# Reordering a down projection's operand splits around the next projection's block splits, on one Trainium2 core

## The reference

```python
def swiglu(h, w_gate_up, w_down):
    gu = h @ w_gate_up
    g, u = gu[..., :D_FF], gu[..., D_FF:]
    return (jax.nn.silu(g) * u) @ w_down

def shared_kv(x, kv_norm_g, w_kv_s):
    kv = rms_norm(x, kv_norm_g) @ w_kv_s
    k = kv[..., :H_B * DH_B] ...   # and v from the other half

for i in range(DEPTH):             # DEPTH = 2
    h = rms_norm(x, norm_mix_g[i])
    if i < N_A_LAYERS:  mix = diff_attn_layer(h, ...)
    else:               k_s, v_s = shared_kv(x, ...); mix = stick_breaking_layer(h, k_s, v_s, ...)
    x = x + mix
    x = x + swiglu(rms_norm(x, norm_ffn_g[i]), w_gate_up[i], w_down[i])
```

## Time and profile before

| | |
|---|---|
| time, median of 3 runs (lowest, highest) | 1648.55 us (1645.99, 1650.98) |
| the profiled execution's own time | 1650.5 us |
| its span | 1648.6 us |
| mean granted clock of TensorE | 0.995 |
| PE busy | 1618.5 us (98%) |
| PEld busy | 1486.4 us (90%) |
| DVE busy | 1162.8 us (71%) |
| ACT busy | 753.4 us (46%) |
| POOL busy | 216.5 us (13%) |

### The profile page before, as it was taken

How to read it: one execution, slowest core, us unless ns; L and a number is a source line. 1 busy time by engine, 2 the same in 40 slices (tenths; PEclk the granted TensorE clock), 3 DMA queues, 4 the chain that set the end, 5 groups by cost and what they waited for, 6 DMA issues and landing times.

```text
span 1648.6 us, 31629 instructions
## 1 busy us (share of the span) xinstructions
PE 1618.5 (98%) x13132; PEld 1486.4 (90%) x13132; DVE 1162.8 (71%) x1605; ACT 753.4 (46%) x1264; POOL 216.5 (13%) x191
## 2 busy tenths in 40 slices
PE   9999999999999999999899999999999999999999
PEld 8888766699999999999899897667999999999999
DVE  5765477667984797488786337778679848974874
ACT  6444476765541354144555214657555413531441
POOL 0000000023220011012344100000231200110110
PEclk9999999999999999999999999999999999999999
DMA  7133899931222122222234458997412221221222
GB/s 286 67 118 138 349 419 419 419 132 52 103 77 103 52 82 99 76 78 90 90 115 169 165 212 349 419 418 314 167 59 95 90 90 52 103 102 53 78 103 90
DMA packets 40252, 267.54 MB, mean 162 GB/s; under 512 B 4400, under 2 KB 4784, under 8 KB 10928
## 3 DMA queue, kind: packets, MB, share of 16 engines
q1 hardware_dynamic: 36720, 252.95, 39.8%
q0 software_dynamic: 3392, 12.58, 2.1%
HBM read 249.79 MB, written 15.73 MB: 161 GB/s over the span
## 4 chain that ended last, share of the span: by engine, by line
PE 84%; DVE 8%; DMA 3%; ACT 3%; issue 3%; SPq 0%; DVEq 0%; ACTq 0%
PE ps L812 29%; PE ps L608 25%; PE ps L278 4%; PE ps L279 4%; PE ps L280 4%; PE ps L1285 3%; PE ps L1344 2%; PE ps L1226 2%; DVE s_lo L761 2%; PE ps L1263 2%; PE ps L635 2%; PE ps L1248 2%; DMA kv<-in_v_a 1%; DMA xT<-in_v_a 1%; DVE t L775 1%
## 5 line engine op out<-in xcount | busy, mean ns | idle before, releaser
L757 ACT ACTIVATE s_hi<-t 128x512 fp32r<-128x512 f32 x192 | 119.2, 626 | 156.1 <-PE ps L812 69.9
L812 PE MATMUL ps<-hs_hi,s_hi 128*128 128x320 f32 x576 | 179.1, 311 | 2.8 <-DVE hs_lo L443 2.8
L812 PE MATMUL ps<-hs_hi,s_lo 128*128 128x320 f32 x576 | 178.0, 309 | 0.0
L812 PE MATMUL ps<-hs_lo,s_hi 128*128 128x320 f32 x576 | 178.0, 309 | 0.0
L256 DVE TENSOR_TENSOR w_lo<-w_raw,w_hi 128x2048 fp32r<-128x2048 f32 x51 | 117.8, 2310 | 67.4 <-ACT w_hi L240 67.4
L240 ACT ACTIVATE w_hi<-w_raw 128x2048 fp32r<-128x2048 f32 x51 | 97.4, 1910 | 148.1 <-PE ps L608 122.2
L608 PE MATMUL ps<-gu_hi,w_hi 128*128 128x320 f32 x692 | 159.1, 311 | 4.8 <-DVE xT L1959 4.6
L608 PE MATMUL ps<-gu_hi,w_lo 128*128 128x320 f32 x692 | 158.5, 310 | 0.0
L608 PE MATMUL ps<-gu_lo,w_hi 128*128 128x320 f32 x692 | 158.5, 310 | 0.0
L761 DVE TENSOR_TENSOR s_lo<-t,s_hi 128x512 fp32r<-128x512 f32 x192 | 146.7, 770 | 7.8 <-ACT s_hi L757 7.0
L757 ACT ACTIVATE s_hi<-w_raw 128x512 fp32r<-128x512 f32 x144 | 90.0, 625 | 90.5 <-PE ps L608 48.6
(11 more groups left out here) (325 smaller groups left out, 4060.8 us busy)
## 6 DMA issues: line engine op xcount, KB each, us to landing
w_raw<-in_w SPq DMA_DIRECT2D x99, 1024.0 KB, 4.8
kv<-in_k_a SPq DMA_DIRECT2D x12, 1024.0 KB, 17.7
kv<-in_v_a SPq DMA_DIRECT2D x12, 1024.0 KB, 17.9
kv<-in_v_s SPq DMA_DIRECT2D x12, 1024.0 KB, 14.0
kv<-in_k_s SPq DMA_DIRECT2D x12, 1024.0 KB, 16.0
xT<-in_k_a SPq DMA_DIRECT2D x8, 1024.0 KB, 17.8
xT<-in_k_s SPq DMA_DIRECT2D x8, 1024.0 KB, 12.0
work<-in_v_a SPq DMA_DIRECT2D x7, 1024.0 KB, 16.5
```

Source lines behind the costliest of these rows:

```text
L757: nc.scalar.activation(s_hi[i][:, :, :], factor(j % 2, i), ACT.Copy).then_inc(hi_done, 1)
L812: last = nc.tensor.matmul(ps[:, bank[i], 0:HALF], w[:, p, :], m[:, p, :], start=(i < 3 and p == 0 and a == 0), stop=(p == 3 and a == 2), s ...
```

## The change

In the last down projection of layer 0, units 0 and 1 no longer split the weights of the unit after next (L240 on ACT, L256 on DVE) ahead of the odd tile's combinations. They do it in their middle: ACT after `ho_hi` and before `hs_hi`, DVE after `ho_lo` and before `hs_lo`. After unit 2 the four key blocks, which were made in one piece ahead of pair 2's odd tile, are spread: on ACT blocks 0 and 1 between `ho_hi` and `hs_hi` and blocks 2 and 3 behind it; on DVE block 0 between `ho_lo` and `hs_lo`, block 1 behind it, and blocks 2 and 3 after the first tile of unit 3 (the last even tile, 6). `sums12` of the keys goes behind pair 1. In all three uses of `norm_pool`, POOL's addition of the squares of tile 6 (and so of tile 7) waits for all 16 low parts of the norm. No computation is added or removed, and PE's list and the loads' list are the same as before.

```diff
@@ odd_dve @@
-            def odd_dve(self, dve, p):
+            def odd_dve(self, dve, p, between=None):
@@
                 nc.vector.scalar_tensor_tensor(ho_lo[:, p, :], o, go, ho_hi[:, p, :].bitcast(F32),
                                                ALU.mult, ALU.subtract).then_inc(mix["lo"], 1)
+                if between is not None:
+                    between()
                 dve.wait_ge(mix["hi"], 4 * m + 4)
@@ norm_pool @@
                 nm.even_pool(pool, p)
+                if p == 3:
+                    pool.wait_ge(mix["lo"], 16 * (nm.i + 1))
                 nm.add(pool, 2 * p)
@@ down_act @@
                 nm.even_act(act, j)
                 if j < 2:
-                    split_hi(act, ph, j + 2, j % 2)
+                    nm.odd_act(act, j, lambda: split_hi(act, ph, j + 2, j % 2))
                 elif j == 2:
-                    first_his(act, "ks", range(4))
-                nm.odd_act(act, j, (lambda: copy_p1(act, N_F, 0)) if j == 3 else None)
+                    nm.odd_act(act, j, lambda: first_his(act, "ks", (0, 1)))
+                    first_his(act, "ks", (2, 3))
+                else:
+                    nm.odd_act(act, j, lambda: copy_p1(act, N_F, 0))
@@ down_dve @@
                     nc.vector.tensor_tensor(x, y, x, ALU.add).then_inc(x_done, 1)
+                    if j == 3 and n == 0:
+                        gu_lo_block(dve, "ks", 0, 2)
+                        gu_lo_block(dve, "ks", 0, 3)
                 if j < 2:
-                    split_lo(dve, ph, j + 2, j % 2)
+                    nm.odd_dve(dve, j, lambda: split_lo(dve, ph, j + 2, j % 2))
+                elif j == 2:
+                    nm.odd_dve(dve, j, lambda: gu_lo_block(dve, "ks", 0, 0))
+                    gu_lo_block(dve, "ks", 0, 1)
+                else:
+                    nm.odd_dve(dve, j)
                 if j == 1:
                     sums12(dve, "ks", 0)
-                if j == 2:
-                    for i in range(4):
-                        gu_lo_block(dve, "ks", 0, i)
-                nm.odd_dve(dve, j)
```

## The result

| | before | after |
|---|---|---|
| median, 18 runs each (us) | 1648.63 (1645.99 to 1650.98) | 1650.72 (1649.17 to 1652.80) |
| profiled execution: time, span (us), clock | 1650.5, 1648.6, 0.995 | 1650.46, 1648.5, 0.997 |
| forecast (us) | | 1649.0 (1644.2 to 1652.3) |

The ratio of after to before is 1.0014, with a 95% interval from 1.0008 to 1.0021: 1.3 to 3.5 us slower. That is within the 0.3% that the forecast counted as no change, and yet it is a loss, 1.7 us more than the 0.4 of the forecast. The time lies in the stated range, which is 8 us wide, but 0.2 outside the narrower one of the forecast itself (1647.5 to 1650.5), between it and rival B. The two profiled executions, of the same length, don't show the loss.

What follows compares the result with a forecast made beforehand. PE, busy 98%, gains only from shorter waits, unit 3's set by DVE's row and POOL's turns. Keys -0.2 and two feed-forward parts +0.6 give +0.4 on 1650.5, moved to the median 1648.55: 1649.0 us, range 1644.2 to 1652.3.

Steps and rivals of the forecast that it cites:

- rival B: All three norms: the two additions at the end make the total late and bound them; +4.6, say 1652 us; chance 0.14.
- Pairs 0 and 1: Last down projection: POOL's turns delay unit 0's row by 0.6 and unit 1's by 0.8; the projection ends 0.4 later.
- Pair 2 and the keys: Ahead of the key sum: last odd tile +1.35, L434 freed of a turn -1.26; `hs_lo` 0.1 later, keys taken as -0.2.
- Feed-forward: Each of two parts: 0.5 wait for `hs_lo` goes, 0.9 wait for total comes, half-sum 0.3 later; +0.3 each.
- Moved to the median of the runs, 1648.55: Last step: the +0.4 reckoned on the profiled 1650.5 is carried over to the runs' median, giving 1649.0 us.
- the clock's second fall: Keys, behind pair 3's wait: costs 1.6 in the profile; if it recurs keys are 0.1 later, if not 0.6 earlier.
- A: POOL gets no turn in a run of DVE instructions; unit 3 starts 2.2 earlier, say 1644.7 us; chance 0.16.
- C: Waits are fixed by tiles and squares, so nothing moves by more than 0.2; 1648.5 us; chance 0.08.

Runs made afterwards that it cites:

- e5: The changed kernel with POOL's new wait for the low parts kept in the norm of the keys only; 1650.04 us.
- e2: The kernel before, in its own order, with POOL's new wait for the low parts added alone; 1649.31 us.
- e1: The changed kernel without POOL's new wait for the low parts, so the new order alone; 1649.95 us.
- e0: The kernel before run and profiled again without an edit; median 1648.62 us, profiled execution 1648.4 us.
- e3: The changed kernel with POOL's additions of tiles 1 to 5 in the key norm cut from 640 to 8 columns; 1645.01 us.
- e4: The kernel before with POOL's additions of tiles 1 to 5 in the key norm cut from 640 to 8 columns; 1646.40 us.
- e8: The changed kernel with all seven additions of the key norm on DVE and no POOL wait for low parts in any norm; 1646.84 us.
- e10: The kernel before, in its own order, with all seven additions of the key norm on DVE; 1648.94 us.
- e9: The kernel of e8 with the additions of tiles 6 and 7 in the feed-forward norms also on DVE; 1645.11 us.

## Why the forecast came out as it did

**Pairs 0 and 1: right.** Forecast: unit 2 waits 1.2, found 1.12; `hs_lo` 2.5 twice, found 2.53; L434 of pair 1 1.75, found 1.75; unit 3's wait 4.4, found 4.18. The three turns are where the forecast had them. What it left open of the Trainium skill's rule on the shared ports (SBUF — State Buffer, Who interferes with whom), who is next when both queue, the runs answer with one exception: POOL's waiting instruction, ahead of DVE's next one with two on-chip inputs. In e5 it was once the other way round.

**Pair 2 and the keys: right in its steps.** L434 of pair 3 fell to 0.49; the wait for the last `hs_lo` was to be 1.6 and is 1.29; the wait for the total was to be 0.9 if the clock didn't fall again, and it didn't: 0.67. The held-up block split ahead of unit 3's first tile is there too (2.07), though e5 shows that it needn't be. For that case the forecast had -0.6 against its profile, and the distance is 58.08 against 58.72: -0.64.

**Feed-forward: right in kind, 0.1 too low in size.** Forecast +0.3 each, measured +0.41 (e2: +0.42, e1: +0.01). The wait for the total is 0.65 instead of 0.9, and it doesn't matter: the second turn acts through the half-sum, as the forecast said, and that comes 0.42 later instead of 0.3.

**The step that failed is the last one, "Moved to the median of the runs, 1648.55".** With the clock's second fall counted as it came out, the steps give -0.6 + 0.8 = +0.2 on the profiled 1650.5, and the changed kernel's profiled execution took 1650.46. That this is so close is in part luck: behind the sum the changed kernel takes 0.7 more up to the split at 903, and in layer 1's attention 1.0 less. But 1.6 of that 1650.5 was an open slow stretch at the keys, which e0, near the median, doesn't have, and the changed kernel can't win back what isn't lost. Against e0 the same rows read +0.98 + 0.82 = +1.8, and the runs +2.1; with e5's profile of the same code at the keys they would read +0.12 + 0.82 = +0.9, so how well 1.8 fits is luck too. That most runs of before are like e0 is inferred from their times. The profile did warn of it: 1650.5 was 2 us above the median that stood beside it, and the forecast used the difference as a mere offset.

**Rivals.** A's turns-free picture is excluded by `hs_lo` at 2.53, and shown as a possible one by e3. B's waits for the total came in all three norms, at 0.65 to 0.67 instead of up to 1.4, but in the feed-forward parts they aren't the bound; the half-sum is. C is excluded by the same `hs_lo`, and by parts that move and cancel (e3, e4).

**The cause of the loss.** The new order by itself is worth about 2 us where no addition takes a turn between DVE's instructions (e8 against e10: 2.1, and 1.9 by the keys; e3 against e4 gives 1.4, which by itself is within the intervals). It moves `hs_lo` and L434 to where POOL's additions fall due, and the additions then cost 5.7 instead of 2.3 (e3 and e4). The waits behind the low parts add 0.8 in the feed-forward norms. What the medians can't settle is how the 2.1 of the changed kernel divides: e1 and e2 give +1.3 and +0.6, but both intervals take in no change.

## What to carry to other kernels

Before an order is changed around a bound DVE, write down when each POOL instruction falls due: it nearly always took its whole turn in front of the next DVE instruction with two on-chip inputs, and here the turns that the new order drew on itself (5.7 - 2.3 = 3.4 us) were worth more than the order (2). A small elementwise sum that DVE does in half of POOL's time belongs in DVE's own row, best where DVE is idle (e9), rather than on POOL beside a DVE that is on the path. Where POOL's sum falls due in DVE's idle time or ahead of a PSUM reader, moving it gains nothing (e10).

If the profiled execution differs from the median by more than the effect that is forecast, profile the kernel again before moving a difference from the one to the other; a part's distance between two fixed rows, compared in several profiles, shows which of them has the difference. And when two waits follow each other, price the one that ends last: here a wait of 0.65 for the total cost nothing, because the half-sum behind it came later still.

## What the runs showed of the hardware

- DVE and POOL take turns instruction by instruction. An addition of 128x640 takes 1.57 us on POOL and 0.82 on DVE; due inside a DVE instruction it showed 1.80 to 2.68 and held the next one by 1.3 to 1.4 (2.53 against 1.15 in e8 for the same `hs_lo`). Once, in e5, the next one went first, in its usual 0.69, and the addition showed 2.76; the same code in the changed kernel had the turn, 0.43 us after the start of the same instruction in both.
- After an idle time of 4.0 us the clock stayed at its lower level until 823.39 in one execution of the kernel before and some 2.5 us less in another. After 1.81 us it fell in one; after 1.89 (e1) and 1.29 (after) it didn't. Falls of this kind move the time of one and the same kernel by 1.6 us, and where a fall lands behind a wait that another wait follows soon, the second wait hides it.
